# Sample tokens out of the dense expert stages of a one-core decoder layer, by gathers and dots

## The chip, the cores and the metric

The kernel runs on one NeuronCore of one Trainium2 chip. The metric is the device time of one execution in microseconds (us). A core has TensorE (PE, with its weight loads as PEld), VectorE (DVE), ScalarE (ACT), GpSimd (POOL) and SyncE (SP), which here only issues DMAs. The engines run their own instruction streams and meet at semaphores.

## The reference

One layer of a hybrid decoder for 256 prompt tokens and 32 sample tokens (8 sequences of 4), D = 1024. The first half (projection, pooling mixer, sparse attention, output projection) is not touched. The second half is a product-key expert retrieval over 128 x 128 experts, each one row of U and one row of V:

```python
def peer(h, w_pq, sub_keys, expert_u, expert_v):
    q = (hf @ w_pq).reshape(N, PEER_HEADS, 2, PEER_HALF)
    s = jnp.einsum('nhcd,hckd->nhck', q, sub_keys)
    sv, si = lax.top_k(s, PEER_TOPK)                      # 8 heads, 16 of 128 keys, twice
    cand = sv[:, :, 0, :, None] + sv[:, :, 1, None, :]    # 256 sums, the best 16 of them
    fv, fi = lax.top_k(cand.reshape(N, PEER_HEADS, 256), PEER_TOPK)
    ...
    a = gelu(einsum('td,ted->te', xt, expert_u[et]))      # 128 experts of each token
    return einsum('te,ted->td', gt * a, expert_v[et])
```

A token uses 128 of the 16384 experts, with gates g from a softmax. Everything is float32.

## The kernel before

NT = 288 tokens are held transposed, h2 as [128, KC = 8, 288]. The experts are computed **densely**, for all tokens: they come in NU = 128 blocks of 128 experts (expert i * 128 + j is row j of block i), first all of U, then all of V. Products are float32 made from single-pass float32r matmuls: every operand is split into hi (the float32r rounding) and lo (the rest), and hi x hi, hi x lo and lo x hi are summed in PSUM.

- **U stage** (`prod_u`, L878): unit n takes block n of U, 8 chunks x 3 matmuls of 128 x 128 by 288 columns. SP loads the block (512 KB) into `w_raw`, a ring of RING = 4, when unit n - 4 is done. ACT (`split_w`, by `next_w`, L962) makes `w_hi`, POOL (`low_w`, L1340) `w_lo`. ACT applies Gelu to the product.
- **Routing** on DVE runs beside units 0 to 35: the top-16 searches (`best16`, `route`), index look-ups (`look_up`, L1576 to L1582) and gates (`slots`, L1600). Ahead of unit SLOTS_AT = 36 PE waits for `slots_ready` and turns them; ACT copies them to iT, jT (block and row of each chosen expert) and wT (its gate), one column per token. Units 0 to 15 (FRONT) also carry the rest of the routing's queries on PE.
- **Spread steps**, G_AT = 44 to G_END: with step k DVE (`hots`, L1611 to L1615) makes one-hot matrices of NB = 4 tokens, PE (`spread`, L889) multiplies them to the gate of each expert for these tokens, and DVE (`weigh`, L1634 and L1635) brings it into `store` [128, block, token], over the stored Gelus of earlier blocks. `gate` (L1623) does it for the block just made. 288 / 4 = 72 steps, one to a unit; the last 12 U units have none.
- **V stage** (`prod_v`, L944): unit v takes block v of V (load `load_v`, L441) and the row v of `store`, again split: ACT `high_ag`, DVE `low_ag` (L1655, ring of 2). 24 matmuls, chunk c into PSUM bank (c + 6) % 8, which accumulates over all 128 units.
- **End**: DVE adds x_res (the saved x1) to the 8 banks, SP writes y.

The order of work is written out by hand on each engine: unit v - 2 of V being done (`prod_done`) is what lets SP issue the load of V unit v + 2, ACT make ag_hi of v + 2, and DVE make ag_lo of v. Queues are in order.

## Time and profile before

| | us |
|---|---|
| runs | 1138.78, 1139.28, 1141.84; median 1139.28 |
| profiled execution, its own time | 1139.06 |
| its span in the trace | 1136.9 |
| PE busy, DVE busy, ACT busy, POOL busy | 1113.7, 616.2, 430.9, 706.6 |
| DMA moved | 186.62 MB, 164 GB/s |

How to read the rows below: in a table by stage a row is from:to, its length, then for PE, PEld, DVE, ACT and POOL the busy time with the number of instructions, then the granted TensorE clock (1.00 is full speed, 2.4 GHz), the DMA engines' busy share and GB/s. A timeline row is start, duration, engine, line, operation, output<-inputs, shape, count, and in brackets the idle time before it with what ended it. A row of waits has the waiting line <- what it waited for: total us, times, longest. Matmul records overlap (their ends are modelled), so spacing is read from their starts.

### The profile page before, as it was taken

What the parts mean: (1) busy time and instruction counts of PE and PEld (TensorE: products, weight loads), DVE (VectorE), ACT (ScalarE), POOL (GpSimd) and SP (SyncE); (2) the same over time, 40 slices, a digit from 0 to 9 for tenths busy, and PEclk for the clock granted to TensorE, in tenths of its full rate; (3) what the DMA queues carried; (4) which work ended last, traced back from release to release, by engine and by line L of the source; (5) the groups of instructions that cost most, each with busy time, mean ns of one, the idle gap of its engine ahead of it and who ended that gap; (6) DMA issues with size and microseconds to landing.
All of it is one profiled execution on the core that took longest, in us unless ns stands there. A gap on an engine that the chain in (4) does not pass through costs nothing.

```text
span 1136.9 us, 24346 instructions
## 1 busy us (share of the span) xinstructions
PE 1113.7 (98%) x8263; PEld 1045.3 (92%) x8263; DVE 616.2 (54%) x1327; ACT 430.9 (38%) x750; POOL 706.6 (62%) x406
## 2 busy tenths in 40 slices
PE   7999998999999999999999999999999999999998
PEld 3448887899999999999999999999999999999998
DVE  2659999299998166666666671332222322222332
ACT  2133231343454433333333334444444444444442
POOL 4643434065776755555555557777777777777775
PEclk9999999999999999999999999999999999999999
DMA  9444577177654544444444445445555545444554
GB/s 334 121 115 130 169 260 265 66 274 256 206 160 137 167 130 129 126 128 126 127 127 128 128 128 160 154 166 166 166 166 166 165 162 165 161 166 161 164 166 174
DMA packets 64503, 186.62 MB, mean 164 GB/s; under 512 B 9157, under 2 KB 21069, under 8 KB 64068
## 3 DMA queue, kind: packets, MB, share of 16 engines
q1 hardware_dynamic: 59356, 178.60, 48.6%
q0 software_dynamic: 3824, 6.97, 2.0%
q10 hardware_dynamic: 1280, 0.53, 0.2%
q8 instruction: 22, 0.36, 0.1%
q14 instruction: 21, 0.17, 0.0%
HBM read 183.23 MB, written 3.00 MB: 164 GB/s over the span
## 4 chain that ended last, share of the span: by engine, by line
PE 78%; DVE 20%; DMA 1%; ACT 1%; issue 1%; DVEq 0%; SPq 0%
PE psum L944 36%; PE psum L878 25%; PE psum L889 6%; PE psum L493 4%; DVE top L1411 3%; DVE work_s L1412 2%; DVE rwork L1529 1%; DVE cand L1547 1%; PE psum L702 1%; PE psum L729 1%; DVE hit L1576 1%; DVE picked L1579 1%; DVE slots L1582 1%; DVE si L1535 1%; DVE si L1528 1%; PE psum L509 1%
## 5 line engine op out<-in xcount | busy, mean ns | idle before, releaser
L1340 POOL TENSOR_TENSOR w_lo<-w_raw,w_hi 128x1024 fp32r<-128x1024 f32 x256 | 614.5, 2402 | 316.3 <-ACT w_hi L962 316.3
L962 ACT ACTIVATE w_hi<-w_raw 128x1024 fp32r<-128x1024 f32 x256 | 271.7, 1061 | 238.4 <-DMA w_raw<-expert_v 224.7
L878 PE MATMUL psum<-h_hi,w_hi 128*128 128x288 f32 x1024 | 310.1, 303 | 0.0
L944 PE MATMUL psum<-ag_hi,w_hi 128*128 128x288 f32 x1024 | 301.4, 294 | 1.3 <-DVE ag_lo L1655 1.3
L878 PE MATMUL psum<-h_lo,w_hi 128*128 128x288 f32 x1024 | 302.6, 295 | 0.0
L878 PE MATMUL psum<-h_hi,w_lo 128*128 128x288 f32 x1024 | 302.1, 295 | 0.0
L944 PE MATMUL psum<-ag_hi,w_lo 128*128 128x288 f32 x1024 | 301.8, 295 | 0.0
L944 PE MATMUL psum<-ag_lo,w_hi 128*128 128x288 f32 x1024 | 301.5, 294 | 0.0
L1655 DVE TENSOR_TENSOR ag_lo<-store,ag_hi 128x288 fp32r<-128x288 f32 x128 | 121.1, 946 | 284.1 <-PE psum L944 282.9
L878 PEld LDWEIGHTS psum<-h_hi,w_hi 128*128 128x128 f32 x1024 | 192.8, 188 | 1.6 <-issue 1.6
L944 PEld LDWEIGHTS psum<-ag_hi,w_hi 128*128 128x128 f32 x1024 | 192.0, 188 | 1.5 <-issue 1.5
L878 PEld LDWEIGHTS psum<-h_hi,w_lo 128*128 128x128 f32 x1024 | 193.2, 189 | 0.0
L878 PEld LDWEIGHTS psum<-h_lo,w_hi 128*128 128x128 f32 x1024 | 193.1, 189 | 0.0
L944 PEld LDWEIGHTS psum<-ag_hi,w_lo 128*128 128x128 f32 x1024 | 192.1, 188 | 0.0
L944 PEld LDWEIGHTS psum<-ag_lo,w_hi 128*128 128x128 f32 x1024 | 192.0, 188 | 0.0
L1183 ACT ACTIVATE psum<-psum 128x288 f32<-128x288 f32 (+36 forms) x84 | 24.7, 294 | 211.3 <-PE psum L878 211.3
L1634 DVE COPY store<-psum 128x336 f32<-128x336 f32 (+35 forms) x72 | 25.9, 360 | 121.3 <-PE psum L889 121.3
L889 PE MATMUL psum<-i_hot,j_hot 128*128 128x128 f32 x576 | 75.8, 275 | 0.0
L889 PEld LDWEIGHTS psum<-i_hot,j_hot 128*128 128x128 f32 x576 | 71.4, 191 | 0.0
L340 POOL DMA_DIRECT2D v_cache<-cache_v x64 | 34.2, 534 | 56.9 <-issue 52.1
L729 PE MATMUL psum<-h,w_slice 128*128 128x256 f32 x256 | 60.1, 388 | 0.1
L729 PEld LDWEIGHTS psum<-h,w_slice 128*128 128x128 f32 x256 | 48.2, 194 | 7.5 <-issue 1.4
(261 smaller groups left out, 1058.4 us busy)
## 6 DMA issues: line engine op xcount, KB each, us to landing
w_raw<-expert_ut SPq DMA_DIRECT2D x128, 512.0 KB, 3.6
w_raw<-expert_v SPq DMA_DIRECT2D x128, 512.0 KB, 3.3
w_slice<-w_pq_cols SPq DMA_DIRECT2D x32, 512.0 KB, 5.6
w_most<-w_in_blocks SPq DMA_DIRECT2D x8, 699.0 KB, 12.8
w_slice<-w_o_half SPq DMA_DIRECT2D x8, 512.0 KB, 4.2
v_cache<-cache_v POOLq DMA_DIRECT2D x64, 64.0 KB, 3.3
w_o_sb<-w_o_half SPq DMA_DIRECT2D x8, 512.0 KB, 8.0
kT<-cache_kt SPq DMA_DIRECT2D x44, 64.0 KB, 2.0
```

The costliest lines, as they stand in the source:

```text
L340: eng.dma_start(dst[:, bass.ds((4 * i + (first + u)) * width, width)], cache[0, bass.ds(pg[u], 1), :, :].rearrange("a p d -> (a p) d")).th ...
L493: return pe.matmul(psum[:, 4 + (i + 1) % 4, 0:ZQ], hT[:, k, t * P:(t + 1) * P], w_cols(j, k), start=(k == 0), stop=(k == KC - 1))
L729: mm = pe.matmul(psum[:, r % 2, 0:SEQ], w_slice[:, (KC + r) % SLICES, k, :], h2[:, k, 0:SEQ], start=(k == 0), stop=(k == KC - 1))
L878: mm = pe.matmul(psum[:, 2 + s, 0:NT], a[:, s, c, :], b[:, c, :], start=(i == 0), stop=(i == 3 * KC - 1))
L889: mm = pe.matmul(psum[:, 6 + s % 2, b * NU:(b + 1) * NU], j_hot[:, s % 2, b, :], i_hot[:, s % 2, b, :], start=True, stop=True, skip_group_ ...
L944: mm = pe.matmul(psum[:, (c + 6) % 8, 0:NT], a[:, s, c, :], b, start=(first and i == 0), stop=(last and i == 2), skip_group_check=True)
L962: return act.activation(out, in_, ACT.Copy)
L1183: a = act.activation(psum[:, 2 + s, 0:done], psum[:, 2 + s, 0:done], ACT.Gelu)
L1340: pool.tensor_tensor(w_lo[:, s], w_raw[:, s], w_hi[:, s].bitcast(F32), ALU.subtract).then_inc(S["w_lo_ready"], 1)
L1411: settle(dve.max(best, left))
L1634: dve.tensor_copy(part[:, n:NU], g[:, n:NU])
L1655: dve.tensor_tensor(ag_lo[:, s % 2, :], store[:, bass.ds(v, 1)].rearrange("p a t -> p (a t)"), ag_hi[:, s, :].bitcast(F32), ALU.subtract). ...
```

## The change

The 32 sample tokens leave the dense units; SEQ = 256 columns are left in `store`, the products, `ag_hi` and `ag_lo`, and 64 spread steps. What the samples need is computed from gathered rows, token by token (u = 0 to 31):

- PE turns the samples' h2 to rows in FRONT (`h_turn`), ACT copies them to `h_rows`, SP saves them in DRAM (`h_save`). DVE makes the expert numbers `eidx` from iT and jT.
- U: POOL fetches the token's 128 rows of U by index, one to a partition (`fetch_u`, 512 KB); SP loads the token's h row to all 128 partitions (`load_h`, read 128 times from h_save); DVE multiplies and sums (`dot`). Token u's dot stands at unit DOT_AT: 48, 54, ... 102 in the spread steps, then 110, 114, ... 194 over U units and V units 2, 6, ... 66.
- V: after the last dot ACT applies Gelu, DVE makes 32 diagonal blocks (`a_diag`); `fetch_v` fetches the V rows into four buffers, PE sums them in four column groups (`expert_rows`), two tokens ahead of every third V unit from v = 74 to 119. ACT and PE turn the sum back, DVE adds it.
- From unit LO_FROM = 112 on (the last 16 U units and all of V) `w_lo` is made by DVE, in `low_w` between its other work; POOL makes it up to unit 111 and issues the fetches.
- Loops of SP, PE, ACT and DVE from unit 44, 108 or V on are written out. y has bank halves (`y_bank`). Some semaphores of the second norm are shared; POOL's h_lo waits for pnew_ready, and the samples' h_hi and h_lo are gone.

The diff, without renamed semaphores and new signatures:

```diff
-    store = take("store", [P, NU, NT])
+    store = take("store", [P, NU, SEQ])
+    rows_in = take("rows_in", [P, 4, D])
...
-    ag_hi = at("ag_hi", cur[0], [P, RING, NT], F32R)
-    ag_lo = at("ag_lo", cur[0] + RING * NT, [P, 2, NT], F32R)
...
+    H0 = cur[0]
+    h_hi = take("h_hi", [P, KC, SEQ], F32R)
+    h_lo = take("h_lo", [P, KC, SEQ], F32R)
+    cur[0] = H0
+    x_res = take("x_res", [P, KC, NT])
+    a_diag = take("a_diag", [P, NS, NS])
+    eye = take("eye", [P, NS, NS], BF16)
+    y_rows = take("y_rows", [P, 2, P])
...
-    G_STEPS = NT // NB
+    G_STEPS = SEQ // NB
...
+    LO_FROM = G_END + RING
+    DOT_AT = tuple(G_AT + 4 + 6 * u if u < 10 else G_END + 2 + 4 * (u - 10) for u in range(NS))
+    GELU_AT = DOT_AT[-1] + 3
+    DIAG_AT = GELU_AT + 2
+    ROW_AT = tuple(DIAG_AT + 3 + 3 * (u // 2) for u in range(NS))
...
+    def y_bank(c):
+
+        return psum[:, (6, 6, 7, 7, 0, 1, 4, 5)[c], (c % 2 if c < 4 else 0) * SEQ:(c % 2 + 1 if c < 4 else 1) * SEQ]
...
+                if n == 8:
+                    sp.wait_ge(S["rows_copied"], 2)
+                    sp.dma_start(h_save, h_rows[:]).then_inc(S["h_saved"], 16)
...
-            with sp.Fori(FRONT // RING + 1, NU // RING) as m:
+            with sp.Fori(FRONT // RING + 1, G_AT // RING) as m:
                 for s in range(RING):
                     sp.wait_ge(S["prod_done"], RING * m + (s - RING + 1))
                     load_u(RING * m + s, s)
...
+            def load_h(u):
+
+                if u == 0:
+                    sp.wait_ge(S["eidx_ready"], 1)
+                if u >= 2:
+                    sp.wait_ge(S["dots_done"], u - 1)
+                sp.dma_start(rows_in[:, 2 + u % 2, :], h_save[u:u + 1, :].to_broadcast([P, D])
+                             ).then_inc(h_wide_in[u % 2], 16)
+
+            for n in range(G_AT, LAST):
+                sp.wait_ge(S["prod_done"], n - RING + 1)
+                if n < NU:
+                    load_u(n, n % RING)
+                else:
+                    load_v(n - NU, n % RING)
+                if n in DOT_AT:
+                    load_h(DOT_AT.index(n))
+                if n == NU + 2 * RING:
+                    sp.dma_start(x_res[:], x1_save).then_inc(S["x_res_in"], 16)
...
+            def h_turn(half):
+
+                pe.wait_ge(S["h2_s_ready"], 1)
+                if half:
+                    pe.wait_ge(S["rows_copied"], 1)
+                for c in range(4):
+                    mm = tr(psum[0:NS, 1, c * P:(c + 1) * P], h2[:, 4 * half + c, SEQ:NT])
+                mm.then_inc(S["rows_turned"], 1)
...
+            def low_in(n):
+
+                if n < LO_FROM:
+                    pe.wait_ge(S["w_lo_ready"], n + 1)
+                else:
+                    pe.wait_ge(S["w_lo_dve"], n - LO_FROM + 1)
+
+            def prod_u(s, n, free=True, late=False):
                 pe.wait_ge(S["w_hi_ready"], n + 1)
-                pe.wait_ge(S["w_lo_ready"], n + 1)
+                if late:
+                    low_in(n)
+                else:
+                    pe.wait_ge(S["w_lo_ready"], n + 1)
...
@@ -891,7 +957,6 @@
                 mm.then_inc(S["g_psum"], 1)
 
             pe.wait_ge(S["h_lo_p"], 1)
-            pe.wait_ge(S["h_lo_s"], 1)
...
+                if n in (3, 6):
+                    h_turn(n // 3 - 1)
...
+            for n in range(G_END, NU):
+                prod_u(n % RING, n, late=True)
+
+            def prod_v(v, first=False, last=False):
+
+                s = v % RING
+                pe.wait_ge(S["w_hi_ready"], NU + v + 1)
+                low_in(NU + v)
                 pe.wait_ge(S["ag_hi_ready"], v + 1)
                 pe.wait_ge(S["ag_lo_ready"], v + 1)
+                if first:
+                    pe.wait_ge(S["g_done"], G_STEPS)
...
+            def expert_rows(u):
...
+                if u == 0:
+                    pe.wait_ge(S["diag_a_ready"], 1)
+                pe.wait_ge(row_in[u % 4], 16 * ((NS // 2 if u % 4 < 2 else 0) + u // 4 + 1))
+                for j in range(4):
+                    mm = pe.matmul(psum[32 * j:32 * j + 32, 2, 0:2 * P], a_diag[:, u, :],
+                                   rows_in[:, u % 4, j * 2 * P:(j + 1) * 2 * P], start=(u == 0), stop=(u == NS - 1),
+                                   tile_position=(0, 32 * j), skip_group_check=True)
+                mm.then_inc(S["rows_done"], 1)
+
+            for v in range(NU):
+                for u in range(NS):
+                    if ROW_AT[u] == NU + v:
+                        expert_rows(u)
+                if v == NU - 3:
+                    pe.wait_ge(S["rows_copied"], 3)
+                    for a in range(2):
+                        mm = tr(psum[:, 3, a * P:(a + 1) * P], y_rows[:, a, :])
+                    mm.then_inc(S["rows_turned"], 1)
+                prod_v(v, first=(v == 0), last=(v == NU - 1))
 
         @block.scalar
         def _(act):
@@ -1082,8 +1164,8 @@
                 act.wait_ge(S["x1_prompt"], i + 1)
                 act.activation(sq2[:, c, 0:SEQ], xT[:, c, 0:SEQ], ACT.Square).then_inc(S["sq2_ready"], 1)
 
-            act.wait_ge(S["rstd2_half"], 1)
-            act.activation(rstd_a[:, 0:SEQ], rstd_b[:, 0:SEQ], ACT.Sqrt).then_inc(S["rstd2_root"], 1)
+            act.wait_ge(S["rstd_half"], 2)
+            act.activation(rstd_a[:, 0:SEQ], rstd_b[:, 0:SEQ], ACT.Sqrt).then_inc(S["rstd_root"], 1)
...
+                if n in (3, 6):
+                    half = n // 3 - 1
+                    act.wait_ge(S["rows_turned"], half + 1)
+                    copy(h_rows[:, 4 * P * half:4 * P * (half + 1)], psum[0:NS, 1, :]).then_inc(S["rows_copied"], 1)
                 if n == 13:
                     act.wait_ge(S["rs_s_psum"], 4)
+                    act.wait_ge(S["h_saved"], 16)
                     copy(sr_s[:].rearrange("p a b -> p (a b)"), psum[:, 0, :]).then_inc(S["sr_s_copied"], 1)
...
+            for v in range(NU):
+                if v + 2 < NU:
+                    high_ag((v + 2) % RING, v + 2, v >= 2)
+                if v + 3 < NU:
+                    next_w(v % RING, (NU + v) // RING, NU + v)
+                if NU + v == GELU_AT:
+                    act.wait_ge(S["dots_done"], NS)
+                    act.activation(a_s[:, :], dots[:, :], ACT.Gelu).then_inc(S["a_s_ready"], 1)
+                if NU + v == ROW_AT[-1] + 1:
+                    act.wait_ge(S["rows_done"], NS)
+                    copy(y_rows[:].rearrange("p a b -> p (a b)"), psum[:, 2, 0:2 * P]).then_inc(S["rows_copied"], 1)
...
-            pool.tensor_tensor(h_lo[:, :, 0:SEQ], h2[:, :, 0:SEQ], h_hi[:, :, 0:SEQ].bitcast(F32), ALU.subtract
-                               ).then_inc(S["h_lo_p"], 1)
+            pool.wait_ge(S["pnew_ready"], 2)
+            pool.tensor_tensor(h_lo[:], h2[:, :, 0:SEQ], h_hi[:].bitcast(F32), ALU.subtract).then_inc(S["h_lo_p"], 1)
...
+            for n in range(RING):
+                low_w(n, n)
+            with pool.Fori(1, G_AT // RING) as m:
                 for s in range(RING):
                     low_w(s, RING * m + s)
+
...
+            def fetch_u(u):
+
+                if u == 0:
+                    pool.wait_ge(S["eidx_ready"], 1)
+                if u >= 2:
+                    pool.wait_ge(S["dots_done"], u - 1)
+                pool.indirect_dma_start(rows_in[:, u % 2, :], None, u_table,
+                                        bass.IndirectOffsetOnAxis(ap=eidx[:, u:u + 1], axis=0)
+                                        ).then_inc(row_in[u % 2], 16)
+
+            def fetch_v(u):
+
+                if u < 4:
+                    pool.wait_ge(S["dots_done"], NS)
+                else:
+                    pool.wait_ge(S["rows_done"], u - 3)
+                pool.indirect_dma_start(rows_in[:, u % 4, :], None, v_table,
+                                        bass.IndirectOffsetOnAxis(ap=eidx[:, u:u + 1], axis=0)
+                                        ).then_inc(row_in[u % 4], 16)
+
+            for n in range(G_AT, LO_FROM):
+                low_w(n % RING, n)
+                for u in range(NS):
+                    if DOT_AT[u] == n + 4:
+                        fetch_u(u)
+            for u in range(NS):
+                if DOT_AT[u] >= LO_FROM + 4:
+                    fetch_u(u)
+            for u in range(NS):
+                fetch_v(u)
 
         @block.vector
         def _(dve):
@@ -1465,12 +1577,12 @@
...
+            dve.wait_ge(S["x1_saved"], 16)
+            dve.scalar_tensor_tensor(eidx[:, :], iT[:, SEQ:NT], float(NK), jT[:, SEQ:NT], ALU.mult, ALU.add
+                                     ).then_inc(S["eidx_ready"], 1)
...
+            def dot(u):
+
+                dve.wait_ge(row_in[u % 2], 16 * (u // 2 + 1))
+                dve.wait_ge(h_wide_in[u % 2], 16 * (u // 2 + 1))
+                dve.scalar_tensor_tensor(rows_in[:, u % 2, :], rows_in[:, u % 2, :], 1.0, rows_in[:, 2 + u % 2, :],
+                                         ALU.mult, ALU.mult, accum_out=dots[:, u:u + 1]).then_inc(S["dots_done"], 1)
+
+            def low_w(n):
+
+                s = n % RING
+                dve.wait_ge(S["w_hi_ready"], n + 1)
+                dve.tensor_tensor(w_lo[:, s], w_raw[:, s], w_hi[:, s].bitcast(F32), ALU.subtract
+                                  ).then_inc(S["w_lo_dve"], 1)
+
+            def low_ag(v, free=True):
+
+                dve.wait_ge(S["ag_hi_ready"], v + 1)
+                if free:
+                    dve.wait_ge(S["prod_done"], v + (NU - 1))
+                dve.tensor_tensor(ag_lo[:, v % 2, :], store[:, v, :], ag_hi[:, v % RING, :].bitcast(F32), ALU.subtract
+                                  ).then_inc(S["ag_lo_ready"], 1)
...
+                if n in DOT_AT:
+                    dot(DOT_AT.index(n))
+            for n in range(G_END - 1, NU):
+                gate(n % RING, n, G_STEPS)
+                if n >= NU - 2:
+                    low_ag(n - (NU - 2), False)
+                if n + 3 >= LO_FROM:
+                    low_w(n + 3)
+                if n >= G_END and n in DOT_AT:
+                    dot(DOT_AT.index(n))
+            low_w(NU + 3)
+            for v in range(2, NU):
+                low_ag(v)
+                if v + 2 < NU:
+                    low_w(NU + v + 2)
+                if v == 2:
+                    settle(dve.tensor_tensor(eye[:], bc(iota16[:, 0:NS], 1, NS), bc(iota16[:, 0:NS], 2, NS),
+                                             ALU.is_equal))
+                if NU + v in DOT_AT:
+                    dot(DOT_AT.index(NU + v))
+                if NU + v == DIAG_AT:
+                    dve.wait_ge(S["a_s_ready"], 1)
+                    settle(dve.tensor_tensor(a_s[:, :], a_s[:, :], wT[:, SEQ:NT], ALU.mult))
+                    dve.tensor_tensor(a_diag[:], eye[:], bc(a_s[:, :], 2, NS), ALU.mult
+                                      ).then_inc(S["diag_a_ready"], 1)
+                if v == NU - 1:
+                    dve.wait_ge(S["x_res_in"], 16)
+                    dve.wait_ge(S["rows_turned"], 3)
+                    x_s = x_res[:, :, SEQ:NT].rearrange("p (j a) t -> p a j t", a=2)
+                    dve.tensor_tensor(x_s, x_s, psum[:, 3, 0:2 * P].rearrange("p (a j t) -> p a j t", a=2, t=NS),
+                                      ALU.add).then_inc(S["y_added"], 1)
```

## Rows read from the trace of the kernel before

**Rows 1.** The page's head.
```profile
span 1136.9 us, 24346 instructions
```

**Rows 2.** By stage: units 36 to 43, spread steps, last U units, V.
```profile
365.70:391.20 25.50, 25.50 (x188) 25.50 (x188) 3.77 (x6) 10.64 (x19) 15.67 (x7) 0.97 0.48 143
391.20:685.40 294.20, 294.20 (x2307) 294.20 (x2305) 194.32 (x423) 103.08 (x217) 174.03 (x73) 1.00 0.43 129
685.40:723.70 38.30, 38.30 (x290) 38.30 (x289) 7.27 (x15) 16.88 (x24) 27.64 (x12) 1.00 0.54 165
725.30:1132.60 407.30, 407.26 (x3072) 407.08 (x3072) 121.53 (x135) 174.90 (x253) 302.38 (x126) 1.00 0.50 165
```

**Rows 3.** Waits, 232 to 394 us and in V.
```profile
PE psum L477 <- DVE slots L1600: 2.3, 1, 2.3
...
ACT w_hi L962 <- DMA w_raw<-expert_v: 224.7, 125, 3.0
```

**Rows 4.** PE's timeline: 128x256 in column groups, and 32 columns by 128-column weights.
```profile
218.79 3.66 PE L791 MATMUL psum<-w_o_sb,catT 128*32 128x256 f32 x64
...
225.74 1.87 PE L807 MATMUL psum<-sq,ones 128*128 128x32 f32 x16
```

**Rows 5.** Matmuls of L944 and L889: duration min/median/max in ns, first and last start.
```profile
L944 PE MATMUL psum<-ag_hi,w_hi x1024: 288/294/368, 725.3 to 1132.1; 128*128 128x288 f32 x171
...
L889 PE MATMUL psum<-i_hot,j_hot x576: 272/275/275, 394.4 to 685.4; 128*128 128x128 f32 x192
```

**Rows 6.** By stage, the four microseconds after PE's wait before unit 36.
```profile
364.00:366.00 2.00, 2.00 (x10) 1.87 (x10) 0.00 (x0) 1.22 (x12) 0.94 (x1) 0.50 0.04 16
366.00:368.00 2.00, 2.00 (x13) 2.00 (x13) 1.81 (x3) 0.15 (x2) 0.00 (x0) 0.74 0.00 0
```

**Rows 7.** Timeline of DVE in one spread step.
```profile
501.78 0.40 DVE L1634 COPY store<-psum 128x232 f32<-128x232 f32 x1 [1.37 <-PE psum L889]
...
504.25 0.26 DVE L1623 TENSOR_TENSOR store<-psum,store 128x108 f32<-128x108 f32 x1
...
505.87 0.40 DVE L1634 COPY store<-psum 128x228 f32<-128x228 f32 x1 [1.36 <-PE psum L889]
```

**Rows 8.** The page: POOL's transfers of 128 rows, and V's loads (us to landing).
```profile
L340 POOL DMA_DIRECT2D v_cache<-cache_v x64 | 34.2, 534 | 56.9 <-issue 52.1
...
w_raw<-expert_v SPq DMA_DIRECT2D x128, 512.0 KB, 3.3
```

**Rows 9.** Timelines in V around one unit's end (T0 = 900.61).
```profile
900.30 0.30 PE L944 MATMUL psum<-ag_hi,w_hi 128*128 128x288 f32 x1
...
900.61 0.91 DVE L1655 TENSOR_TENSOR ag_lo<-store,ag_hi 128x288 fp32r<-128x288 f32 x1 [2.19 <-PE psum L944]
900.64 0.33 SPq L441 DMA_DIRECT2D w_raw<-expert_v  x1
...
904.01 1.06 ACT L962 ACTIVATE w_hi<-w_raw 128x1024 fp32r<-128x1024 f32 x1 [1.67 <-DMA w_raw<-expert_v]
...
905.15 2.41 POOL L1340 TENSOR_TENSOR w_lo<-w_raw,w_hi 128x1024 fp32r<-128x1024 f32 x1 [0.67 <-ACT w_hi L962]
```

**Rows 10.** DVE's ag_lo: duration min/median/max in ns.
```profile
L1655 DVE TENSOR_TENSOR ag_lo<-store,ag_hi x128: 457/926/2424, 722.7 to 1126.4; 128x288 fp32r<-128x288 f32 x128
```

**Rows 11.** DVE's timeline: a 1024-element op with its successor, and the first ag_lo.
```profile
197.17 1.22 DVE L1493 TENSOR_TENSOR log_s<-log_s,psum 128x1024 f32<-128x1024 f32 x1 [1.01 <-PE psum L754]
198.31 0.15 DVE L1495 TENSOR_TENSOR log_s<-log_s,psum 128x4 f32<-128x4 f32 x1
...
722.67 2.41 DVE L1655 TENSOR_TENSOR ag_lo<-store,ag_hi 128x288 fp32r<-128x288 f32 x1 [0.91 <-ACT ag_hi L962]
```

**Rows 12.** DMA from 897 to 909 us, 40 slices: busy tenths and GB/s.
```profile
DMA  0000067989600009779981000093999610005669
GB/s 14 0 0 0 0 123 273 355 314 410 260 14 0 0 0 150 177 259 396 369 355 41 0 0 0 0 205 82 382 328 437 246 68 0 0 0 68 150 246 369
```

More of the change, by code:

```diff
@@ L153, in hybrid_kernel @@
     top8 = take("top8", [P, 8])
+    eidx = take("eidx", [P, NS], U32)
+    dots = take("dots", [P, NS])
+    a_s = take("a_s", [P, NS])
     F0 = cur[0]
@@ L291, in hybrid_kernel @@
     x1_save = nc.dram_tensor("x1_save", [P, KC, NT], F32, kind="Internal").ap()
+    h_save = nc.dram_tensor("h_save", [NS, D], F32, kind="Internal").ap()
     S = Named(nc, ctx)
     w_slice_in = [ctx.enter_context(nc.semaphore(f"w_slice_in{i}")) for i in range(SLICES)]
+    h_wide_in = [ctx.enter_context(nc.semaphore(f"h_wide_in{i}")) for i in range(2)]
+    row_in = [ctx.enter_context(nc.semaphore(f"row_in{i}")) for i in range(4)]
     w_in_ring = [ctx.enter_context(nc.semaphore(f"w_in_ring{i}")) for i in range(RING)]
@@ L943, in prod_v @@
                     for a, b in ((w_hi, ag_hi[:, s, :]), (w_hi, ag_lo[:, s % 2, :]), (w_lo, ag_hi[:, s, :])):
-                        mm = pe.matmul(psum[:, (c + 6) % 8, 0:NT], a[:, s, c, :], b, start=(first and i == 0), stop=(last and i == 2), skip_group_check=True)
+                        mm = pe.matmul(y_bank(c), a[:, s, c, :], b, start=(first and i == 0 and c not in (1, 3)),
+                                       stop=(last and i == 2), skip_group_check=True)
                         i += 1
@@ L949, in prod_v @@
                     mm.then_inc(S["prod_done"], 1)
-            for s in range(RING):
-                prod_v(s, s, first=(s == 0))
-            with pe.Fori(1, NU // RING - 1) as m:
-                for s in range(RING):
-                    prod_v(s, RING * m + s)
-            for s in range(RING):
-                prod_v(s, NU - RING + s, last=(s == RING - 1))
+            def expert_rows(u):
[17 more added lines that the diff above has]
+                prod_v(v, first=(v == 0), last=(v == NU - 1))
         @block.scalar
@@ L1183, in gated @@
                 a = act.activation(psum[:, 2 + s, 0:done], psum[:, 2 + s, 0:done], ACT.Gelu)
-                if done < NT:
-                    a = act.activation(store[:, n, done:NT], psum[:, 2 + s, done:NT], ACT.Gelu)
+                if done < SEQ:
+                    a = act.activation(store[:, n, done:SEQ], psum[:, 2 + s, done:SEQ], ACT.Gelu)
                 a.then_inc(S["act_ready"], 1)
@@ L1616, in hots, with gate @@
                                   ).then_inc(S["hot_ready"], 1)
-            def gate(s, n, steps, done=NT):
+            def gate(s, n, steps, done=SEQ):
                 dve.wait_ge(S["act_ready"], n - (G_AT - 1))
@@ L1644, in _ @@
                 weigh(k)
-            gate(RING - 1, G_END - 1, G_STEPS)
-            with dve.Fori(G_END // RING, NU // RING - 1) as m:
-                for s in range(RING):
-                    gate(s, RING * m + s, G_STEPS)
-            def low_ag(s, v, free=True):
-                dve.wait_ge(S["ag_hi_ready"], v + 1)
-                if free:
-                    dve.wait_ge(S["prod_done"], v + (NU - 1))
-                dve.tensor_tensor(ag_lo[:, s % 2, :],
-                                  store[:, bass.ds(v, 1)].rearrange("p a t -> p (a t)"),
-                                  ag_hi[:, s, :].bitcast(F32), ALU.subtract).then_inc(S["ag_lo_ready"], 1)
```

113 lines of the change are left out of this document (37 added, 76 removed).

## The prediction

> **What bounds the kernel now.** I read the page first for its span [rows 1], then the busy times by stage [rows 2]. From the routing's end (365.7 us) to the last matmul (1132.6 us) PE is busy in every microsecond: 25.5 us for units 36 to 43, 294.2 us for the 72 units with a spread, 38.3 us for the last 12 U units, 407.3 us for the 128 V units. These stretches, 1.6 us between U and V and 4.3 us of tail add up to the span of 1136.9. Before 365.7 it is not PE: it waited 2.3 us for DVE's last routing step [rows 3], and DVE works through its routing without needing PE's unit pace. So whatever PE saves in units 0 to 35 becomes a longer wait at that place; only what comes after it counts.
>
> A matmul of 288 columns takes 407.3 / 3072 = 132.6 ns from start to start [rows 2], a unit of 24 3.18 us. A step with its spread takes 294.2 / 72 = 4.086 us, so the spread's eight records cost 0.904.
>
> **What the matmuls give.** At 256 columns the spacing is 117.8 ns if it goes with the columns (132.6 x 256/288), and 119.3 if the excess over 288 / 2.4 GHz = 120 ns stays. I take 118.5, a unit of 2.845 us. Bounds: the sixteen 32-column matmuls with 128-column weights took (1.87 - 0.27) / 15 = 107 ns each [rows 4, 5], which streaming cannot explain, so the weights set a floor near 107; and at worst nothing changes (132.6).
>
> [...]
>
> Stages after the routing: units 36 to 43, 8 x 2.845 = 22.8 (was 25.5). Spread steps are now 64, 64 x (2.845 + 0.904) = 239.9; the other 20 U units 56.9. Together 319.6 against 358.0: **38.4 us gained**. Units 0 to 35 would save 36 x 0.34 = 12 us, and get nothing: DVE's routing is not touched, PE waits 14 us instead of 2.3. The clock was granted at 0.50 and 0.74 in the 4 us after the present wait [rows 6]; a longer wait costs that again, not more.
>
> Hidden in U: the two turns of h2 and the h_save transfer stand in PE's new wait. A spread step's DVE work runs from 501.78 to 504.51, 2.73 us, and then DVE waits 1.36 for the next spread [rows 7]. The step shrinks to 3.75, so 1.0 us of it is idle; a dot (1.14 us, below) every sixth step overruns by 0.1 and is made up in the next. If that cover went, ten dots would cost 11 us. ACT and POOL stay under 1.6 and 2.4 us per step. A row fetch on POOL: the nearest row is 0.53 us for a 128-row transfer, 1.42 with the idle time before each [rows 8]. In a spread step w_hi of unit n + 3 follows the Gelu of unit n, so w_lo is done some 0.4 + 1.06 + 2.4 = 3.9 us after unit n, and PE wants it two steps and a spread later, after 8.1: with POOL's own idle time of 1.3 a fetch of up to 5 us, once in six steps, would be free.
>
> **What moving w_lo does to V: the chain that takes PE's place.** Take the moment T0 at which unit v-2 is done, 0.31 us after the next unit's first matmul started (900.30, 900.61) [rows 9]. At T0 SP issues the load of unit v+2; ACT starts w_hi of it at T0 + 3.40 (904.01), ends at 4.46, and its reader starts 0.08 later (905.15). Now that reader is POOL, and w_lo is wanted three units later: there is slack. In the new program DVE does low_ag(v), low_w(v+2), low_ag(v+1) in this order. So low_ag(v+1), which PE wants only **two** units after T0, stands behind the wait for that load. A 1024-element two-source op occupies DVE 1.14 us (197.17 to 198.31), an ag_lo of 288 columns took 0.457 at its shortest, so 0.42 at 256, and PE started 0.22 after an ag_lo ended (722.67 + 2.41 = 725.08, to 725.3) [rows 5, 10, 11]. From T0 to the start of unit v+1: 3.40 + 1.06 + 0.08 + 1.14 + 0.42 + 0.22 = 6.32. Since T0 is one unit and 0.31 behind the start of v-2, three units take at least 2.845 + 0.31 + 6.32 = 9.475, or **3.158 us a unit** where matmuls alone would take 2.845 and the old loop takes 3.18. V's plain units gain nothing to speak of.
>
> A dot (1024 elements, two sources, 1.14 us) stands in the same queue every fourth unit up to v = 66. The slowest path is one three-unit step over the dot and one plain unit: (9.475 + 1.14 + 2.845) / 4 = 3.365 us a unit. That the data of a dot is late I exclude in the sum: its fetch is triggered two dots earlier, its h row two units earlier.
>
> The V rows: 16 pairs of expert_rows, 16 records a pair, 64 such column-group records took 3.66 us [rows 4], so 0.92 us a pair, most of it inside PE's wait for DVE. Their two fetches bring 1 MB per three units. A 512 KB load holds the DMA engines about 1.7 of its 3.3 us (the busy run of slices of 0.3 us in each period) [rows 8, 12], the queues share them, and overlap delays a load by 0 to 1.6 us; the fetches start when a pair is done, between two loads, so I take 0.4: (9.475 + 0.4) / 3 = 3.29 us a unit.
>
> V's sum: units 0 to 2, 8.5 + 1.1 for eye; 64 dot units 215.4; 67 to 73, 22.1 + 2.5 (burst of four fetches, by 1.6 us twice at most) + 1.2 (a_diag); 48 row units 158.0; the last six, 4 x 3.158 + 2 x 2.845 = 18.3. **427.1 against 407.3: 19.8 lost.** Handover U to V: 1.0 for 1.6, since the ag_lo of 2.41 us there [rows 11] ran beside POOL's w_lo, which is gone. Tail 4.0 for 4.3 (256 columns).
>
> **Sum.** 365.7 + 22.8 + 239.9 + 56.9 + 1.0 + 427.1 + 4.0 = 1117.4. The profiled execution took 2.2 us more than its span and the median is 0.2 above it: **1120 us**.
>
> **Rivals.**
> No chain: DVE's order does not bind, PE alone sets V. V is then 128 x 2.845 + 16 x 0.92 = 378.9, the time 1072. For it: DVE is busy only 121.5 of 407 us in V [rows 2]. Against: the wait is for the load, not for DVE's speed, and ACT waits 224.7 us for those loads today [rows 3]. Chance 7%.
> The gap sinks to the weights' floor: at 107 ns a unit is 2.57 us, spread steps 3.47, V's three-unit step 9.20, and the same sum gives 20.6 + 222.3 + 51.4 + 411.6 for the stages, 1079. For it: with 256 columns the streaming (107 ns at 2.4 GHz) and the floor are equal. Against: 288 columns cost 10% more than their streaming, and nothing says that this ends. 8%. [...]
> Slower, by row traffic: gathers and broadcasts lengthen the loads of V. Each 0.1 us of landing costs 64 x 0.025 + 48 x 0.033 = 3.2 us; a full overlap of 1.6 us gives 1120 + 25.6 + 19.2 = 1165. It decides from 0.6 us per load: below that faster, above slower. For it: the loads are exactly the chain's longest part, and traffic per unit grows by half to two thirds. Against: the engines are busy 0.50 of V [rows 2], and the phases worked out above mostly miss. 15%.
> Broadcast slow: 128 reads of one 4 KB row of h_save, on SP's own queue ahead of the next load. No row shows such a read. At the rate of other loads it is 1.6 us and hidden; at 5 us the following load comes 2 us late in each dot period, some 14 us in all, about 1134; at 16 us it holds all 32 dots by some 13 each, above 1500. 12%.
> The matmuls do not shorten (something else than columns sets 132.6): G 64 x 4.086, the other U units 3.18, V (6.63 + 3.18) / 3 and (9.81 + 1.14 + 3.18) / 4 a unit: 50 more, 1170. For it: 132.6 is 10% over the streaming of 288 columns, so something else is in it. Against: the 107 ns floor lies far below it. 8%.
>
> **Numbers.** My forecast's case has 50%, with a range of its own from 1108 to 1132 (spacing 117.8 to 119.3: 4 us each way; overlap 0 to 0.8: -6 to +8). Below 1085 lie the no-chain case and part of the floor case, above 1165 the extreme of the broadcast and half of the unshortened case: 1085 to 1165. A change under 0.3% (3.4 us) cannot be told from none. Faster: 46 of the 50, the 7 and the 8, and 2 of the transfer cases, 0.63. Within: 0.08. Slower: 0.29.
>
> **What would show it.** PE matmuls 118 ns apart, spread steps of 3.75 us; a wait of some 14 us for DVE slots before unit 36; in V, PE waiting for DVE's ag_lo or w_lo in most units, DVE's idle time ended by ACT's w_hi, periods of 3.16, 3.37 and 3.29 us; landings of 3.3 us for w_raw. If V shows periods of 2.85 the chain is wrong; if landings are over 3.9 or dots wait for row_in or h_wide, traffic wins. If G steps exceed 3.75 with PE waiting for hot_ready or w_lo, the hidden dots or fetches were not hidden.

## The result, and the profile after

The changed kernel takes 1155.97 us (median of 4 runs, 1152.1 to 1158.44), the kernel before 1139.93 in the same rounds: the ratio is 1.0136, with a 95% interval from 1.0104 to 1.0168. So it is 1.4% slower, where 1120 us and a gain were forecast. The profiled execution took 1152.1 us, 3.9 below the median, with a span of 1150.4; stages are compared on it, and some 4 us of the difference to the forecast are in no trace.

The head of the page, the end of its chain by engine, and four groups of its costliest instructions (busy us, mean ns, then idle time before them and what ended it):

```profile
span 1150.4 us, 22909 instructions
...
PE 1064.8 (93%) x8465; PEld 977.3 (85%) x8465; DVE 749.1 (65%) x1500; ACT 425.2 (37%) x745; POOL 426.7 (37%) x325
...
PE 54%; DVE 21%; DMA 15%; issue 5%; ACT 4%; POOL 0%; DVEq 0%; SPq 0%; POOLq 0%
...
L1011 PE MATMUL psum<-ag_hi,w_hi 128*128 128x256 f32 x1024 | 298.4, 291 | 57.3 <-DVE ag_lo L1770 54.7
L1762 DVE TENSOR_TENSOR w_lo<-w_raw,w_hi 128x1024 fp32r<-128x1024 f32 x144 | 176.6, 1227 | 249.6 <-ACT w_hi L1044 248.7
L1441 POOL DMA_INDIRECT rows_in<-expert_u,eidx x32 | 31.1, 970 | 252.7 <-DVE rows_in L1755 250.9
L1451 POOL DMA_INDIRECT rows_in<-expert_v,eidx x32 | 36.1, 1127 | 162.1 <-PE psum L1025 129.8
```

PE is no longer busy in every microsecond: its first matmuls of V's units (L1011 now, L944 before) waited 54.7 us for DVE's ag_lo, and DVE's w_lo waited 248.7 us for ACT's w_hi. The waits of the whole run say the rest (us in total, times, longest):

```profile
ACT w_hi L1044 <- DMA w_raw<-expert_v: 285.7, 120, 7.2
DVE w_lo L1762 <- ACT w_hi L1044: 248.7, 119, 6.0
PE psum L1011 <- DVE ag_lo L1770: 54.7, 49, 4.2
PE psum L522 <- DVE slots L1712: 11.5, 2, 6.9
```

Before, ACT waited 224.7 us for these loads with 3.0 at the longest [rows 3]. The stages, as windows (length; busy time of PE, its weight loads, DVE, ACT, POOL; granted clock; DMA share; GB/s): spread steps, last U units, V up to the last dot, up to the first row sum, the row sums, the last units.

```profile
384.00:625.00 241.00, 241.00 (x2050) 241.00 (x2049) 202.19 (x395) 90.63 (x193) 165.01 (x75) 1.00 0.56 188
625.00:683.40 58.40, 57.80 (x483) 57.63 (x481) 34.47 (x49) 28.18 (x41) 9.50 (x7) 1.00 0.76 265
683.50:931.00 247.50, 209.74 (x1618) 203.35 (x1619) 128.04 (x174) 92.86 (x137) 16.99 (x18) 0.97 0.65 217
931.00:956.00 25.00, 20.33 (x156) 19.99 (x156) 10.77 (x16) 8.19 (x13) 2.80 (x3) 0.93 0.63 223
956.00:1119.00 163.00, 149.39 (x1342) 137.43 (x1340) 70.69 (x91) 61.38 (x90) 32.15 (x28) 1.00 0.74 236
1119.00:1147.00 28.00, 27.36 (x222) 26.35 (x218) 13.80 (x23) 9.83 (x15) 0.00 (x0) 1.00 0.41 123
```

U came out as forecast: V starts at 683.4 us for 725.3 before [rows 5]. V takes 463.4 us, where it took 407.3 [rows 2] and was forecast at 427.1. That is the whole miss: +36.3 in V, -2.9 ahead of it, -0.4 in the tail; with the 3.9 between this execution and the median, the 36 us.

What it waits for stands in the chain that ended last, followed back, here from 971 to 983 us (start, length, what):

```profile
971.74 5.18 DMA w_raw<-expert_v
976.92 0.02 issue
976.95 1.07 ACT w_hi L1044
978.01 0.02 issue
978.04 0.04 DVE w_lo L1762
978.07 1.11 issue
979.18 0.43 DVE ag_lo L1770
979.61 0.14 issue
979.74 3.12 PE psum L1011 x24
982.87 0.02 issue
982.88 4.31 DMA w_raw<-expert_v
```

A load is issued when a unit of PE ends, and lands 5.18 us later; ACT makes w_hi, DVE w_lo (0.04 and the 1.11 called issue), then the ag_lo that stood behind it, and only then PE can do its next unit. The w_lo made here is wanted by a later unit, the ag_lo that waited is wanted now. One turn of this, 11.14 us, is three units. The timeline around a dot (in brackets the idle time before and what ended it) shows the dot in the same queue, between w_lo and ag_lo:

```profile
792.57 1.22 DVE L1762 TENSOR_TENSOR w_lo<-w_raw,w_hi 128x1024 fp32r<-128x1024 f32 x1 [1.34 <-ACT w_hi L1044]
793.71 1.22 DVE L1755 SCALAR_TENSOR_TENSOR rows_in<-rows_in 128x1024 f32<-128x1024 f32 x1
...
794.85 0.42 DVE L1770 TENSOR_TENSOR ag_lo<-store,ag_hi 128x256 fp32r<-128x256 f32 x1
...
795.42 0.36 PE L1011 MATMUL psum<-ag_hi,w_hi 128*128 128x256 f32 x1 [0.95 <-DVE ag_lo L1770]
```

### The profile page after: what moved, and what is told of

Read it like the earlier page. It is cut to its first block, busy times and chain, and to the rows that moved or that the text cites. A ratio compares the mean times of both kernels' runs of the same rounds, so it can differ in the third digit from the quotient of the medians.

```text
span 1150.4 us, 22909 instructions
## 1 busy us (share of the span) xinstructions
PE 1064.8 (93%) x8465; PEld 977.3 (85%) x8465; DVE 749.1 (65%) x1500; ACT 425.2 (37%) x745; POOL 426.7 (37%) x325
## 4 chain that ended last, share of the span: by engine, by line
PE 54%; DVE 21%; DMA 15%; issue 5%; ACT 4%; POOL 0%; DVEq 0%; SPq 0%; POOLq 0%
PE psum L944 23%; PE psum L1011 16%; DMA w_raw<-expert_v 14%; PE psum L955 5%; PE psum L538 4%; ACT w_hi L1044 3%; DVE top L1523 3%; DVE work_s L1524 2%; DVE rwork L1641 1%; DVE cand L1659 1%; DVE ag_lo L1770 1%; PE psum L747 1%; PE psum L774 1%; DVE picked L1691 1%; DVE hit L1688 1%
## 5 line engine op out<-in xcount | busy, mean ns | idle before, releaser
L1011 PE MATMUL psum<-ag_hi,w_hi 128*128 128x256 f32 x1024 | 298.4, 291 | 57.3 <-DVE ag_lo L1770 54.7
L1762 DVE TENSOR_TENSOR w_lo<-w_raw,w_hi 128x1024 fp32r<-128x1024 f32 x144 | 176.6, 1227 | 249.6 <-ACT w_hi L1044 248.7
L1423 POOL TENSOR_TENSOR w_lo<-w_raw,w_hi 128x1024 fp32r<-128x1024 f32 x112 | 268.4, 2400 | 142.7 <-ACT w_hi L1044 142.5
L944 PE MATMUL psum<-h_hi,w_hi 128*128 128x256 f32 x1024 | 297.1, 290 | 1.3 <-issue 1.3
L1011 PE MATMUL psum<-ag_lo,w_hi 128*128 128x256 f32 x1024 | 293.5, 287 | 0.0
L1011 PE MATMUL psum<-ag_hi,w_lo 128*128 128x256 f32 x1024 | 293.4, 287 | 0.0
L944 PE MATMUL psum<-h_lo,w_hi 128*128 128x256 f32 x1024 | 289.9, 283 | 0.0
L944 PE MATMUL psum<-h_hi,w_lo 128*128 128x256 f32 x1024 | 289.9, 283 | 0.0
L1011 PEld LDWEIGHTS psum<-ag_hi,w_hi 128*128 128x128 f32 x1024 | 200.2, 196 | 72.1 <-issue 51.6
L1011 PEld LDWEIGHTS psum<-ag_lo,w_hi 128*128 128x128 f32 x1024 | 200.5, 196 | 0.0
L1011 PEld LDWEIGHTS psum<-ag_hi,w_lo 128*128 128x128 f32 x1024 | 200.2, 196 | 0.0
L944 PEld LDWEIGHTS psum<-h_hi,w_hi 128*128 128x128 f32 x1024 | 196.5, 192 | 3.0 <-issue 2.7
L944 PEld LDWEIGHTS psum<-h_lo,w_hi 128*128 128x128 f32 x1024 | 196.8, 192 | 0.0
L944 PEld LDWEIGHTS psum<-h_hi,w_lo 128*128 128x128 f32 x1024 | 196.4, 192 | 0.0
L1451 POOL DMA_INDIRECT rows_in<-expert_v,eidx x32 | 36.1, 1127 | 162.1 <-PE psum L1025 129.8
L1755 DVE SCALAR_TENSOR_TENSOR rows_in<-rows_in 128x1024 f32<-128x1024 f32 x32 | 60.7, 1897 | 0.0
```

The costliest lines, as they stand in the source:

```text
L944: mm = pe.matmul(psum[:, 2 + s, 0:SEQ], a[:, s, c, :], b[:, c, :], start=(i == 0), stop=(i == 3 * KC - 1))
L1011: mm = pe.matmul(y_bank(c), a[:, s, c, :], b, start=(first and i == 0 and c not in (1, 3)), stop=(last and i == 2), skip_group_check=True)
L1423: pool.tensor_tensor(w_lo[:, s], w_raw[:, s], w_hi[:, s].bitcast(F32), ALU.subtract).then_inc(S["w_lo_ready"], 1)
L1451: pool.indirect_dma_start(rows_in[:, u % 4, :], None, v_table, bass.IndirectOffsetOnAxis(ap=eidx[:, u:u + 1], axis=0)).then_inc(row_in[u % ...
L1755: dve.scalar_tensor_tensor(rows_in[:, u % 2, :], rows_in[:, u % 2, :], 1.0, rows_in[:, 2 + u % 2, :], ALU.mult, ALU.mult, accum_out=dots[: ...
L1762: dve.tensor_tensor(w_lo[:, s], w_raw[:, s], w_hi[:, s].bitcast(F32), ALU.subtract).then_inc(S["w_lo_dve"], 1)
```

## The experiments

Eleven runs were made, of ten edited kernels. V is read from the start of its first matmul to the start of its last; its period over the dots is the time between the first and the last dot in V (L1755) over their 16 intervals of four units, that over the row sums between the first and last pair's first matmul (L1025) over 15 intervals of three units.

| kernel | time, us (runs) | V | four units with a dot | three with a pair |
|---|---|---|---|---|
| changed | 1155.97 (4) | 463.4 | 14.66 | 10.77 |
| e2: no row traffic | 1122.07 (1) | 434.1 | 13.64 | 9.91 |
| e5: no h broadcasts | 1141.9 (1) | 454.7 | 14.17 | 10.63 |
| e6: no fetches | 1124.25 (1) | 435.1 | 13.60 | 9.99 |
| e7, e8: dot ahead of w_lo | 1150.86 (1), 1143.46 (10) | 458.2, 458.6 | 14.04, 14.00 | 11.36, 11.43 |
| e1: w_lo one unit later | 1088.97 (4) | 403.3 | 12.26 | 9.93 |
| e4: e1 without row traffic | 1077.4 (1) | 389.7 | 11.46 | 9.82 |

**e1_later_w: only the order.** Iteration v makes the low part of W of unit v+1 instead of v+2; the one made ahead of the loop goes.

```
-            low_w(NU + 3)
             for v in range(2, NU):
                 low_ag(v)
-                if v + 2 < NU:
-                    low_w(NU + v + 2)
+                if v + 1 < NU:
+                    low_w(NU + v + 1)
```

> The changed kernel with one line moved: in V, VectorE makes w_lo of unit v+1 (not v+2) in iteration v, so its wait for a load no longer stands ahead of low_ag(v+1). The gathers, broadcasts, dots and column-group sums all stay. Theory 1 (the in-order chain load, w_hi, w_lo, ag_lo sets V, and row traffic only makes its load longer): V falls from 463 us to what PE needs, 128 x 2.88 + 16 x 0.9 = 383 to 395, the time from 1156 to 1075 to 1090. Theory 2 (row traffic starves the loads whatever the order): V stays above 440, time 1135 to 1156. Theory 3 (the written-out code makes PE wait for its own instructions): no change, 1156.

1088.97 us, ratio to before 0.9538 (0.9519 to 0.9558). Two of its waits in V, from 684 to 1100 us:

```profile
ACT w_hi L1044 <- DMA w_raw<-expert_v: 224.2, 108, 7.1
...
PE psum L1011 <- DVE ag_lo L1770: 10.3, 15, 1.2
```

The same instructions, one unit later, are worth 67 us against the changed kernel by the medians, and 60 by the two profiled executions, all of it in V. The time is in the expected range; V is not (403.3, above 395), and Theory 3 is out, since this code is written out too. DVE's w_lo now meets a load that has had a unit longer, and ag_lo stands behind no recent load. The loads themselves are no earlier: from issue to ACT's start they take 4.4 us over the dots and 4.9 over the row sums on average, where the changed kernel has 4.2 and 4.3 and the kernel before 3.4. So the order does not make the loads faster, it keeps most of their lateness off PE's path.

**e2_no_traffic: only the transfers.** The order of the changed kernel, without the row traffic and without the waits for what is no longer fetched (two more edits of the same kind, not shown); later dots and sums work on stale rows.

```
-                if n in DOT_AT:
+                if n in DOT_AT[:2]:
                     load_h(DOT_AT.index(n))
...
-                    if DOT_AT[u] == n + 4:
+                    if u < 2 and DOT_AT[u] == n + 4:
...
-            for u in range(NS):
+            for u in range(4):
                 fetch_v(u)
```

> The changed kernel without the row traffic after the first two U fetches, h loads and the first four V fetches: later dots and sums work on stale rows (their output is not the reference's), all engine work and VectorE's order stay. Theory 1: V keeps the chain, with landings of 3.4 us: 3.17 us a plain unit, 13.5 us per four dot units, V about 427 us, time about 1120. Theory 2 (traffic alone is the loss): V falls to 385 to 395, time 1080. Theory 3: 1156.

1122.07 us: without the traffic V falls from 463.4 to 434.1 (1120 and 427 were expected). DVE over four units, from the timeline:

```profile
843.12 1.22 DVE L1755 SCALAR_TENSOR_TENSOR rows_in<-rows_in 128x1024 f32<-128x1024 f32 x1
...
844.26 0.42 DVE L1770 TENSOR_TENSOR ag_lo<-store,ag_hi 128x256 fp32r<-128x256 f32 x1
...
855.72 1.23 DVE L1762 TENSOR_TENSOR w_lo<-w_raw,w_hi 128x1024 fp32r<-128x1024 f32 x1 [1.55 <-ACT w_hi L1044]
856.86 1.22 DVE L1755 SCALAR_TENSOR_TENSOR rows_in<-rows_in 128x1024 f32<-128x1024 f32 x1
```

From dot to dot it is 13.74 us here and 13.5 in most of the others, 13.64 on average; the chain as worked out asks 4 x 3.365 = 13.46. So the chain's arithmetic holds over the dots where the loads are left alone. What the changed kernel has above this run, 29 us over V, comes with the transfers; some 5.5 us of it by way of PE's clock, as shown further down. Like e4, e5, e6, e3 and e9 this is a single run.

**e5_no_h and e6_no_fetch: which transfers.** e5 leaves out the h broadcasts alone, e6 the indirect fetches alone, each by its part of the edit of e2.

> The changed kernel without the broadcast loads of h_save after the first two (dots use stale h rows; the sample output is not the reference's). All fetches, dots and VectorE's order stay. The traffic as a whole cost 463 - 434 = 29 us of V (e2_no_traffic). If the broadcast reads are the slow part (same row 128 times, on SP's own queue ahead of the next load): time falls by 15 to 22 us, to 1134 to 1141. If all traffic counts by its bytes: it is a third of the dot stage's extra bytes in V and none of the row stage's: by 8 to 11 us, to 1145 to 1148.

> The changed kernel without the indirect fetches of U after the first two and of V after the first four (stale rows in dots and sums; the sample output is not the reference's). Broadcast loads stay. If the fetches on POOL's queue, sharing the DMA engines with the loads, are the cost: time falls by 18 to 24 us, to 1132 to 1138, most of it in the row stage (units 74 to 118 from 3.6 to 3.2 us). If the broadcast is: by under 10 us.

Without the broadcasts V is 454.7 (9 less), without the fetches 435.1 (28.3 less, of 29.3 for both). The fetches carry nearly all of it; the two do not add up, since removing the broadcasts after the fetches gives only another 1. e5's time lies between its two ranges, its V in the 8 to 11 of the second (the broadcasts are half of the bytes that the dot stage adds in V, though, not a third). e6 saved more than the 18 to 24 expected, and most of it over the dots: 17 us there, 12 over the row sums. Over the dots a fetch and a broadcast move the same 512 KB, and taking out the fetches gives twice what the broadcasts give, so bytes alone do not price them; whether the fetches' queue, their scattered rows or their moment does it was not tried.

**e3_before_dve_w and e9_before_dve_w_next: the order in the old kernel.** The kernel before, with its dense V of 288 columns and no row traffic, but V's low part of W on DVE: e3 in the order v+2, e9 in the order v+1. In the cut the line with a minus is e3's, the one with a plus e9's.

```
                 pe.wait_ge(S["w_lo_dve"], v + 1)       # was w_lo_ready, POOL's
...
                 for s in range(RING):
                     low_ag(s, RING * m + s)
-                    low_w((s + 2) % RING, RING * m + (s + 2))     # e3
+                    low_w((s + 1) % RING, RING * m + (s + 1))     # e9
```

> The kernel before, all 288 tokens dense, loops kept, with one part of the change alone: in V, w_lo on VectorE, made in iteration v for unit v+2 as in the changed kernel. Theory 1: three V units take 3.18 + 0.31 + 6.35 = 9.84 us, 3.28 each for 3.18, V 419 for 407 us, time about 1151. Theories 2 and 3 (order harmless, no traffic, no written-out code here): 1137 to 1140.

> The kernel before with V's low part of W on VectorE as in e3_before_dve_w, but made for unit v+1 instead of v+2 behind the low part of a*gelu of unit v. Theory, the loss of e3 comes from the order alone: V goes back to PE's pace of 3.18 us a unit, 407 us, and the time is 1137 to 1141. Rival, VectorE's share itself costs (the port, or the ag_lo no longer early): V stays at 413 to 420 and the time at 1147 to 1154.

e3 takes 1154.21 us, 13 more than before, e9 1137.78, no more than before, both as the theory of the order had it. DVE's wait for ACT in V, in e3 (first fence) and in e9 (second), with PE's matmuls in e3:

```profile
DVE w_lo L1662 <- ACT w_hi L962: 211.5, 126, 2.5
...
L944 PE MATMUL psum<-ag_hi,w_hi x1024: 288/294/376, 728.4 to 1148.5; 128*128 128x288 f32 x171
```

```profile
DVE w_lo L1662 <- ACT w_hi L962: 97.7, 118, 1.1
```

V is 420 us in e3 and 407 in e9. In the old kernel, moving the operation to DVE costs nothing by itself; the place in DVE's order does.

**f1_later_shift.** e1 with the slot turns and the spread four units later (so that PE does more before it waits for the routing), and twelve dots under the spread.

```
-    SLOTS_AT = 36
-    G_AT = 44
+    SLOTS_AT = 40
+    G_AT = 48
-    DOT_AT = tuple(G_AT + 4 + 6 * u if u < 10 else G_END + 2 + 4 * (u - 10) for u in range(NS))
+    DOT_AT = tuple(G_AT + 4 + 5 * u if u < 12 else G_END + 2 + 4 * (u - 12) for u in range(NS))
```

> The moved line of e1, and the slots and spread steps four units later (SLOTS_AT 40, G_AT 48; 12 dots in the spread steps, five steps apart), to fill PE's wait of 11.5 us for VectorE's routing with four units. If that wait is the loss of the U stage's first half: 11 us under e1_later_w. If spread steps and dots then run into V's start: within 3 us of e1.

1078.32 us, ratio 0.9463 (0.9439 to 0.9488); 11 us below e1, as expected; V starts at 670.1, 13 us earlier than in e1, and PE's wait for DVE's slots is down from 11.5 to 1.2 us. Units 36 to 39 had waited for nothing, only stood behind the turns.

**e7_dot_first, e8_dot_first_again, f2_dot_first: the dot ahead of the wait.** e7 and e8 are one kernel, the changed one with this edit; f2 is f1 with it.

```
                 low_ag(v)
+                if NU + v in DOT_AT:
+                    dot(DOT_AT.index(NU + v))
                 if v + 2 < NU:
                     low_w(NU + v + 2)
...
-                if NU + v in DOT_AT:
-                    dot(DOT_AT.index(NU + v))
```

> The changed kernel with one other line moved: in V the dot stands ahead of low_w of unit v+2 in VectorE's queue, so it runs while VectorE waits for the load anyway. Theory 1: the 1.14 us of a dot leave the chain, once in four of 64 units: 16 x 1.14 = 18 us less, to about 1138. If dots are not on the path (the loads alone are): 1153 to 1158. If the dot's rows are late where it now stands: slower than 1156.

> The changed kernel with the dot ahead of the low part of W of unit v+2 in V (the order of e7_dot_first), timed in rounds since e7 was one look. Theory, chain over the load with the dot in it: the dot then overlaps the wait for the load, its stage of 64 units is 14 to 18 us shorter, and the whole 14 to 18 us under 1156, so 1138 to 1142. Rival, the load is held back by transfers in any order: what the dots give comes back in the rows' stage, as in the one look (9 us longer there), and the time is near 1151.

> f1_later_shift with the dot ahead of low_w in V as well. There low_w of unit v+1 finds its load landed, so the dot stands in nobody's chain; what is left over PE's 384 to 386 us in V (397 in f1) would be late loads. Theory 1: at most 3 us below f1_later_shift (1078), equal to it within noise. If dots still delay ag_lo: 8 us or more below.

e7 took 1150.86 in one run, where 1138 was expected; e8 1143.46 over ten runs (1137.47 to 1149.19), ratio to before 1.0018 (0.9992 to 1.0044). So the edit is worth 12.5 us, a little under the 14 to 18 expected. In the profiles of both the time from V's start to its last dot falls by 15 us, and that over the row sums grows by 9 to 10 (15 x 0.6), though nothing was changed there. Two windows within the row sums of e8:

```profile
980.00:1000.00 20.00, 17.89 (x151) 16.41 (x150) 7.80 (x10) 7.46 (x11) 4.85 (x4) 0.91 0.69 210
...
1020.00:1040.00 20.00, 18.10 (x158) 17.34 (x158) 8.31 (x11) 7.58 (x12) 4.28 (x4) 1.00 0.78 255
```

In the changed kernel the clock was granted in full over this stage, and at 0.97 over the dots; in e8 it is 0.99 over the dots and 0.95 here. Matmuls are further apart at the lower clock (rows below, under PE's clock), and this alone makes 7.0 of the 10 us in e8 and 4.4 of the 9 in e7; of the 15 us gained over the dots in e8, 5.5 are the same effect the other way. Why the waits that go with it move to the row sums is open; whether a fetch now falls elsewhere in the loads' rhythm was not tried.

f2 takes 1067.93 us, ratio 0.9356 (0.9315 to 0.9396), the best of all: 6.4% under the kernel before, 7.6% under the changed one. By the medians it is 10.4 us under f1, where at most 3 were expected; in the two profiled executions it is 3.4, with V at 393.9 for 397.1. f1's four runs lie 9.8 us apart, so whether the dots still delayed ag_lo by more than those 3 is open. Its clock in V and e1's are at 1.00; the window is f2's:

```profile
683.50:931.00 247.50, 242.63 (x2052) 237.46 (x2051) 147.09 (x196) 110.70 (x165) 37.89 (x29) 1.00 0.79 266
```

**e4_no_traffic_later: what traffic costs where no chain binds.** The edits of e1 and e2 together.

> The order of e1_later_w (the low part of W of unit v+1 in iteration v), and only the first two U fetches and h broadcasts and the first four V fetches are issued; the other dots and row sums work on what is there, so the output is not the reference's. Theory, traffic costs by lengthening a chain and costs little where no chain binds: V is PE's own, 128 units of 2.88 and 16 pairs of 0.9, 383 us against 403 of e1, and the time 1069 to 1073. Rival, the loads' residual lateness in e1 (waits of up to 7.1 us for w_raw) is that of the queue itself and not of the rows' transfers: V stays near 400 and the time near 1087.

1077.4 us, where 1069 to 1073 was expected. V's stages up to the first row sum, the row sums, and the rest:

```profile
682.40:897.60 215.20, 213.75 (x1776) 213.26 (x1776) 141.83 (x189) 101.68 (x151) 4.32 (x4) 1.00 0.63 197
897.60:1045.40 147.80, 147.80 (x1332) 136.87 (x1335) 73.69 (x91) 61.45 (x90) 0.00 (x0) 1.00 0.52 161
1045.40:1071.80 26.40, 26.40 (x228) 25.99 (x221) 13.48 (x21) 9.83 (x15) 0.00 (x0) 1.00 0.43 125
```

PE is busy for 388 of the 389.7 us: this is V at PE's own pace. It also gives the price of a pair of row sums that no wait hides: 9.82 - 3 x 2.88 = 1.18 us, where I had 0.92, and with it PE's pace is 128 x 2.88 + 16 x 1.18 = 387.5; of the 6.7 us by which V misses the expected 383, the pairs are 4.5. The traffic costs 403.3 - 389.7 = 13.6 us in this order, for 29.3 in the other.

## Why the prediction was wrong

**Up to V: right.** The spacing, forecast at 118.5 ns within 117.8 to 119.3, is 120: two matmuls of one unit, 24 apart, are 2.88 us apart.

```profile
639.78 0.28 PE L944 MATMUL psum<-h_hi,w_hi 128*128 128x256 f32 x1
...
642.66 0.28 PE L944 MATMUL psum<-h_hi,w_hi 128*128 128x256 f32 x1
```

It is just above the range, and the rivals at 107 and 132.6 are both out. The spread stage was forecast at 239.9 and took 241.0 with ten dots and the fetches in it, so these were hidden, as said. PE waited 11.5 us for DVE's slots (14 forecast): the gain of units 0 to 35 went there. The routing itself ended 4.6 us earlier than before (the slots' last step starts at 359.07 us, it was 363.64), which the sum did not have; the spread stage and the last U units with the handover (58.4 for 57.9) took 1.6 of it back. With 256 columns, ag_lo is 0.42 us as forecast:

```profile
L1770 DVE TENSOR_TENSOR ag_lo<-store,ag_hi x128: 411/419/486, 682.7 to 1141.1; 128x256 fp32r<-128x256 f32 x128
```

**The chain over the load: right in kind, and nearly in size.** V without it is 389.7 (e4), with it and without traffic 434.1 (e2): 44.4 us. The terms gave 427.1 - 378.9 = 48.2, and 39.3 without the 8.9 of traffic in them. A period with a dot was forecast at 13.46 and is 13.64 on average in e2, 13.53 without the first of its 16. The rival without a chain is out for this order, and nearly true for the other (e1's V 403.3, e4's at PE's own pace).

**What failed is the overlap of the transfers**: "I take 0.4" for each load over the row sums, where the bound was 1.6, and nothing over the dots, since "the phases worked out above mostly miss". For the dots' stage no phase had been worked out. The periods are longer than the chain's sum by 14.66 - 13.46 = 1.2 us over the dots and 10.77 - 9.475 = 1.3 over the row sums; against e2, which differs in the traffic alone, by 1.0 (16 times) and 0.86 (15 times), and these make the 29. The loads show it: from issue to ACT's start 4.2 us on average over the dots and 4.3 over the row sums, 3.6 in e2, 3.40 before [rows 9]; 5.18 and 4.31 in the chain's rows above. A wait for a late load counts once in three or four units, so not every load's lateness is on the path. V's miss of 36.3 us is then 16 x 1.2 = 19.2 over the dots, 15 x 0.9 = 13.5 over the row sums, and 3.6 around them. These put into the sum give 1120 + 19 + 14 = 1153.

Not all of this is traffic: e2 without it is at 434.1, and the same terms without overlap and burst give 427.1 - 6.4 - 2.5 = 418.2. Of those 15.9, 6.5 are the row sums, whose period of 9.91 is PE's own (9.82 by e4, above the chain's 9.475: the pair's 1.18 for 0.92, and 2.88 for 2.845); 2.8 are the dots' periods, and 6.6 lie around the changeovers, 2.9 of them PE's clock (below), the rest unexplained. The transfers' part is 29.3, against 8.9 in the sum.

The rival that I gave 15% had the mechanism and the price. Its turning point was 0.6 us a load, and that leaves out the 0.4 that the sum already held: by its own price, 1120 - 6.4 + 32 x 0.8 = 1139, it is 0.8. The outcome is on the slower side of either. I weighed it by the mean DMA share of 0.50 and by a phase from a trace without the new transfers. The phase does not stay: in the changed kernel the 16 periods over the dots run from 13.4 to 16.8 us, in e2 all but the first from 13.4 to 13.7. That a late load shifts the next issue, and with it where the following fetch falls, is how I read this; no run holds the phase fixed. Nor are the DMA engines full: their share is 0.65 and 0.74 in the two long stages.

A fetch is 512 KB. Those of V land 5.8 us after their issue, by the median, and hold POOL for 1.1 us on average (up to 1.8), those of U for 1.0:

```profile
rows_in<-expert_v,eidx POOLq DMA_INDIRECT x32, 5.8
```

The Trainium skill (DMA: Bandwidth & Descriptors, SWDGE vs HWDGE vs iDMA) says that each DMA engine takes turns between the queues that feed it. e6 fits that: without the other queue's transfers V's loads are back at 3.6 us from issue to ACT's start. No run shows the turns themselves.

**Part of it is PE's clock.** Of its two levels, 2.4 and 1.2 GHz, V had the lower one in six stretches, 20.5 us together and 17 of them over the dots, where the mean is 0.97. One of the waits before them, and the stretch that followed, as a window:

```profile
863.64 0.35 PE L1011 MATMUL psum<-ag_hi,w_hi 128*128 128x256 f32 x1 [2.58 <-DVE ag_lo L1770]
...
864.00:867.40 3.40, 3.40 (x18) 3.40 (x18) 2.84 (x4) 2.08 (x4) 0.00 (x0) 0.50 0.05 18
```

Matmuls start 213 ns apart there, for 120, and over the six stretches this adds up to 8.5 us, 7.0 of them over the dots. It was in no term of the sum. e2 has two such stretches, both at changeovers, which cost 2.9, so of the 29 us between e2 and the changed kernel some 5.5 are the clock's. Each of the six came with a wait of PE for ag_lo of 2.2 to 4.2 us, five of them within 1.5 us after it and one just at its end; e1, e4, f1 and f2, whose PE waits for ag_lo are shorter (2.0 us at most), have no such stretch in V. But a wait of 2.2 us at 1045.5 brought none, and e6, with the chain and without the fetches, has a single one. So it goes with the long waits; what decides it is not shown.

**The broadcasts were cheap, though not quick**: 9 us at the most (e5), 1 with the fetches gone. One such read lands 4.4 us after its issue in e6 and 4.8 in e1, so near the rival's case of 5 us, and far from 16; but no dot waited for its h row, and the loads of e6, whose broadcasts stay, are hardly later (3.6 us) than those of e2, where the rival had them 2 us late in each dot period:

```profile
rows_in<-h_save SPq DMA_DIRECT2D x32, 512.0 KB, 4.4
```

## What to carry to other kernels

When an operation moves onto an in-order engine, look at what now stands behind its wait, and ask how old the load is that it waits for: here one unit of distance in the order of DVE's queue was worth 60 to 67 us, and in the old kernel the move itself nothing. Where a chain goes through a load, the transfers added beside it come onto the path, whatever the mean DMA share says: here a period lost about 1 us of the 1.6 that a full overlap could cost. So do not price it near nothing unless something holds the phases apart, and break the chain first (the same traffic cost 29 us with it and 13.6 without). A rival with a price and a turning point worked out deserves a chance by that price, and not by an average.
